# Attention on one core: key tiles turned and multiplied in pairs, reciprocal sums spread through a DRAM row

## The reference

```python
q = concat([q_nope, q_rope])          # (1, 8 heads, 2048, 128 + 64)
k = concat([k_nope, k_rope])          # (1, 8 heads, 2304, 128 + 64): latent and context keys
v                                     # (1, 8 heads, 2304, 128)
s = einsum('bhqd,bhkd->bhqk', q, k) / sqrt(192)
p = softmax(s, axis=-1)
o = einsum('bhqk,bhkd->bhqd', p, v)
y = (o * silu(gate)) @ w_o
```

## Time and profile before

| | us |
|---|---|
| median of 3 timed runs (2950.66 to 2951.75) | 2951.46 |
| the profiled execution | 2949.36 |
| its span, from first to last instruction | 2947.6 |
| attention stage in it, first scores at 572.9, last product at 1942.4 | 1369.5 |
| PE busy over the span | 2873.8 |
| DVE, ACT, POOL busy over the span | 1918.9, 1505.9, 318.3 |

### The profile page before, as it was taken

How to read it: one execution, slowest core, us unless ns; L and a number is a source line. 1 busy time by engine, 2 the same in 40 slices (tenths; PEclk the granted TensorE clock), 3 DMA queues, 4 the chain that set the end, 5 groups by cost and what they waited for, 6 DMA issues and landing times. The chain is left out here.

```text
span 2947.6 us, 42819 instructions
## 1 busy us (share of the span) xinstructions
PE 2873.8 (97%) x14429; PEld 2390.4 (81%) x14429; DVE 1918.9 (65%) x3154; ACT 1505.9 (51%) x3103; POOL 318.3 (11%) x427
## 2 busy tenths in 40 slices
PE   6999999999999999999999999999999999999998
PEld 4888888788888888888888888878878888888787
DVE  6555645476767676776767677653347586965875
ACT  5554646455656565555656555544442323334643
POOL 0000000022122212212221222110000000000000
PEclk9999999999999999999999999999989999999999
DMA  7557564611211211021111211145442333344663
GB/s 272 203 201 261 180 220 159 234 53 34 76 44 43 56 60 57 26 77 44 60 39 60 60 33 54 33 143 171 157 152 78 112 103 101 108 125 132 221 197 119
DMA packets 220342, 335.92 MB, mean 114 GB/s; under 512 B 70080, under 2 KB 131152, under 8 KB 218832
## 3 DMA queue, kind: packets, MB, share of 16 engines
q1 hardware_dynamic: 215504, 324.63, 33.9%
q10 hardware_dynamic: 4608, 8.39, 0.7%
HBM read 235.31 MB, written 97.66 MB: 113 GB/s over the span
## 5 line engine op out<-in xcount | busy, mean ns | idle before, releaser
L1324 DVE TENSOR_TENSOR at_ptlo<-at_T,at_pthi 128x512 fp32r<-128x512 f32 x576 | 396.9, 690 | 304.2 <-ACT at_pthi L1202 301.2
L1186 ACT ACTIVATE at_prob<-at_S,at_nmax 128x512 f32<-128x512 f32 x634 | 407.4, 658 | 343.8 <-DVE at_nmax L1300 322.4
L1202 ACT ACTIVATE at_pthi<-at_T 128x512 fp32r<-128x512 f32 x576 | 349.0, 608 | 208.7 <-PE at_T L1068 208.7
L1289 DVE TENSOR_REDUCE at_mx<-at_S 128x1 f32<-128x512 f32 x634 | 390.6, 631 | 73.8 <-PE at_S L1041 70.7
L1068 PE MATMUL at_T<-ident,at_prob 128*128 128x128 f32 x2304 | 346.5, 273 | 2.6 <-DVE at_ptlo L1324 2.6
L1068 PEld LDWEIGHTS at_T<-ident,at_prob 128*128 128x128 f32 x2304 | 279.9, 141 | 68.1 <-DVE at_ptlo L1324 11.5
L197 PE MATMUL ci_ps<-h1hi,ci_whi 128*128 128x512 f32 x768 | 300.7, 392 | 5.3 <-DVE h1lo L2307 5.3
L198 PE MATMUL ci_ps<-h1lo,ci_whi 128*128 128x512 f32 x768 | 300.0, 391 | 0.0
L199 PE MATMUL ci_ps<-h1hi,ci_wlo 128*128 128x512 f32 x768 | 299.8, 390 | 0.0
L197 PE MATMUL at_O<-at_pthi,at_vhi 128*128 128x512 f32 x576 | 270.1, 469 | 0.6 <-DVE at_og L1338 0.5
L1036 PE MATMUL at_S<-at_khi,at_qhi 128*128 128x512 f32 x634 | 246.1, 388 | 13.0 <-ACT at_prob L1186 10.2
(11 more groups left out here) (294 smaller groups left out, 5818.3 us busy)
## 6 DMA issues: line engine op xcount, KB each, us to landing
fr_w<-in_w_front SPq DMA_DIRECT2D x75, 512.0 KB, 4.3
at_wmod<-in_w_mod SPq DMA_DIRECT2D x32, 512.0 KB, 3.6
ci_band<-in_bands SPq DMA_DIRECT2D x40, 320.0 KB, 3.5
cv_w<-in_cv_w_in SPq DMA_DIRECT2D x24, 512.0 KB, 4.7
fr_w<-in_w_front SPq DMA_DIRECT2D x24, 384.0 KB, 4.0
values<-fr_ob SPq DMA_DIRECT2D x36, 256.0 KB, 2.9
at_vst<-values SPq DMA_DIRECT2D x8, 1152.0 KB, 8.1
fr_w_mod<-in_w_modr SPq DMA_DIRECT2D x17, 512.0 KB, 5.6
```

Source lines behind the costliest of these rows:

```text
L1186: nc.scalar.activation(prob[:, j % 2, i, k], bank(h, j, i, c)[:, 0:k.stop - k.start], ACT.Exp, scale=SCALE, bias=nmax[:, i % 2:i % 2 + 1], ...
L1202: nc.scalar.activation(dst, T[:, (n + SLOTS * j) % 2], ACT.Copy).then_inc(s_hi, 1)
L1289: nc.vector.tensor_reduce(mx[:, i % 2, c:c + 1], bank(h, j, i, c)[:, 0:k.stop - k.start], AXX, ALU.max).then_inc(s_mx, 1)
L1324: nc.vector.tensor_tensor(ptlo[:, kt % 3], T[:, (n + SLOTS * j) % 2], pthi[:, kt % 3].bitcast(F32), ALU.subtract).then_inc(s_lo, 1)
```

## The change

The `den` slot is gone, and so are the diagonals on DVE and POOL, the two matmuls and ACT's copy. `rl` now keeps the four query tiles' reciprocals of a block, and SyncE writes them to a row of 512 numbers in DRAM and, when that has landed, reads the row back to all 128 partitions of `den`. The 18 key tiles are handled as nine pairs: eight transposes in a row (two banks of `T`), then the six products of the pair before. The rings `pthi` and `ptlo` have four tiles where they had three. Pairs stand after chunks 1, 2 and 4 for i = 0 and after chunks 1 and 4 for the other tiles. `sb("apart", ...)` only keeps the addresses of what follows.

```diff
+    PAIRS_AFTER = ((1, 2, NCHUNK - 1),) + ((1, NCHUNK - 1),) * (QT - 1)
+    RING = 4
@@ SyncE
+        def spread_reciprocals(sp, h, j):
+            b = index(h, j)
+            sp.wait_ge(s_recip, b * QT + QT)
+            if not (isinstance(b, int) and b == 0):
+                sp.wait_ge(s_gden, b)
+            sp.dma_start(net.rl_row.rearrange("a (i p) -> p (a i)", p=P), rl[:, j % 2],
+                         allow_slow_non_contiguous=True).then_inc(s_rlst, 16)
+            sp.wait_ge(s_rlst, b * 16 + 16)
+            sp.dma_start(den[:], net.rl_row[0:1, :].to_broadcast([P, BLK])).then_inc(s_den, 16)
...
                     load_gate(sp, nh, nj)
+                spread_reciprocals(sp, h, j)
                 if last and j == 1:
@@ TensorE
-                        if c < len(ns) - TAIL:
-                            step(h, j, ns[c])
-                        if i == 0 and c == TAIL + 1:
-                            values(h, j, 0)
-                    for n in ns[-TAIL:]:
-                        step(h, j, n)
+                        if c in PAIRS_AFTER[i]:
+                            pair(h, j, first_pair[i] + PAIRS_AFTER[i].index(c))
+
+            def pair(h, j, p):
+                for n in (2 * p, 2 * p + 1):
+                    transposes(h, j, n)
+                if p:
+                    for n in (2 * p - 2, 2 * p - 1):
+                        values(h, j, n)
+                elif not (isinstance(h, int) and h == 0 and j == 0):
+                    for n in (NKT - 2, NKT - 1):
+                        values(*((h, j - 1) if j else (h - 1, NBH - 1)), n)
@@ ScalarE, the tail
+                    a, b = tail(i)
+                    high(h, j, a)
                     if with_scores:
                         exponential(nh, nj, i, 0)
-                    high(h, j, ns[-2])
+                        exponential(nh, nj, i, 1)
+                    high(h, j, b)
                     if with_scores:
-                        exponential(nh, nj, i, 1)
                         exponential(nh, nj, i, 2)
-                    high(h, j, ns[-1])
@@ VectorE
-                nc.vector.reciprocal(rl[:, i % 2:i % 2 + 1], lsum[:, i % 2, 7:8]).then_inc(s_recip, 1)
-                dve.wait_ge(s_recip, t + 1)
-                nc.vector.tensor_scalar(dghi[:, j % 2, i * P:(i + 1) * P], net.ident[:], rl[:, i % 2:i % 2 + 1], None,
-                                        ALU.mult).then_inc(s_dghi, 1)
+                nc.vector.reciprocal(rl[:, j % 2, i:i + 1], lsum[:, i % 2, 7:8]).then_inc(s_recip, 1)
@@ GpSimd
-                pool.wait_ge(s_hi, h * (SLOTS * NBH) + (slots.index("den") + 1 + SLOTS * j))
+                pool.wait_ge(s_den, b * 16 + 16)
-            def diagonal_low(h, j, i):
...
```

More of the change, by code:

```diff
@@ L862, in attention @@
     NBH = SEQ // BLK
[L864 to L867, removed]
+    PAIRS_AFTER = ((1, 2, NCHUNK - 1),) + ((1, NCHUNK - 1),) * (QT - 1)
+    first_pair = [sum(len(x) for x in PAIRS_AFTER[:i]) for i in range(QT)]
+    assert sum(len(x) for x in PAIRS_AFTER) == NKT // 2
+    KEARLY, KHIGH = 2, 3
+    RING = 4
     with nc.cleanup_on_exit(), ExitStack() as st:
@@ L882, in attention @@
         lsum = sb("lsum", [P, 2, 8])
[L883 to L886, removed]
+        rl = sb("rl", [P, 2, QT])
+        sb("apart", [P, 5 * 256 - 2 * (QT - 1)])
         den = sb("den", [P, BLK])
@@ L922, in index, with ring, middle, tail @@
             return h * NBH + j
+        def ring(j, n):
+            return (n + NKT * j) % RING
+        def middle(i):
+            return [range(2 * p, 2 * p + 2) for p in range(first_pair[i], first_pair[i] + len(PAIRS_AFTER[i]) - 1)]
+        def tail(i):
+            p = first_pair[i] + len(PAIRS_AFTER[i]) - 1
+            return 2 * p, 2 * p + 1
         def opening(h, j):
@@ L1107, in phase @@
                 for i in range(QT):
-                    ns = list(range(cuts[i], cuts[i + 1]))
                     for c in range(NCHUNK):
@@ L1143, in _ @@
                 phase(HEADS - 1, j, j + 1 < NBH)
-            for n in (SLOTS - 2, SLOTS - 1):
+            for n in (NKT - 2, NKT - 1):
                 values(HEADS - 1, NBH - 1, n)
@@ L1362, in phase @@
                                 denominator(h, j, QT - 1)
-                        if j == NBH - 1 and with_scores and i == 0 and c == 0:
-                            k_low(h + 1, NCHUNK - 1)
+                            if j == 0 and i == 1:
+                                v_low(h, VC - 1)
+                            if j == NBH - 2 and not last and i == QT - 1:
+                                for k in range(KEARLY):
+                                    k_low(h + 1, k)
                     if with_scores:
@@ L1370, in phase @@
                         v_low(h + 1, i - 2)
-                    low(h, j, ns[-2])
-                    if j == NBH - 1 and i >= 2 and with_scores:
-                        denominator(nh, nj, i - 1)
-                    low(h, j, ns[-1])
+                    for n in tail(i):
+                        low(h, j, n)
                     if j == NBH - 2 and not last and i == QT - 1:
```

145 lines of the change are left out of this document (44 added, 101 removed).

## The result

The changed kernel takes 2959.78 us (median of 9 runs, 2954.23 to 2964.15) against 2949.37 us of the kernel before (9 runs, 2948.82 to 2951.75): a ratio of 1.003, with a 95% interval of 1.0022 to 1.0038. It is slower, by 10.4 us, where I had forecast 13.4 us less than 2949.4; it lies above my whole range. The profiled execution took 2961.52 us, of which 2959.4 are its span. The kernel before was timed again with each group of runs; its medians lie between 2948.6 and 2950.43, so that some 1 us between groups means nothing.

What follows compares the result with a forecast made beforehand. Attention was taken as bound by TensorE's instruction stream. From the profiled 2949.4: - 14.7 - 3.5 + 3.0 = 2934.2 us, plus 2.1 for the timed median gives 2936.3, stated as 2936; range 2928 to 2942 (60%).

Steps and rivals of the forecast that it cites:

- The two `den` matmuls: On TensorE's path: removing both saves 0.46 us in each of 32 slots, 14.7 us.
- the 3.5 us of the exponentials: Scores waiting for exponentials at i = 0 of a head's last block: 0.5 us saved in 7 heads, between 0 and 5.
- Pairs in place of single steps: TensorE's fewer changes between transposes and products: taken as 0, with ends of 0 and 23 us gain.
- rival 1: Going from transposes to products really costs 0.08 us, so 23 us more go: 2913 us; chance 13%.
- The tail: Transposes and products before the next scores: a `high` ahead of the exponential on ACT costs nothing, with 0.02 us cover.
- rival 2: ACT's first copy in the tail delays exponentials and scores in 124 tails: 2948 us at 0.1 us beyond the edge; 16%.
- The pair after chunk 1: Its transposes come 4.6 us after the tail's first; the tail's last `low` is done at 3.8, so no cost.
- the DRAM row: Reciprocals written to DRAM and read back: no cost in 31 blocks, since `gden` is wanted one block later.
- The DRAM row's write: SyncE's small write of 128 x 4 pieces of 4 bytes: taken as 3 us, between 2.7 and 10.8.
- Rival 3: The small write takes 10 us or more, hidden in steady blocks but not the last: 2944 us; chance 8%.
- The last block: `og_raw` issued behind the small write makes ACT and PE wait: 3 us lost in sum, between 0 and 11.
- Rival 4: The clock falls in runs of eight transposes; one in ten falling costs 25 us: 2961 us; chance 3%.

Runs made afterwards that it cites:

- Run 7: run 3 plus, in every block, two 512-column matmuls with overwritten results ahead of the transposes of key tile 8: 2932.36 us.
- Run 6: Kernel before with the DRAM row for `den` and run 3's two edits, single steps, three buffers, POOL's gate product also behind `q_low`: 2935.23 us.
- run 5: run 3, with pairs, and POOL's gate product also made to wait until `q_low` is finished: 2921.12 us.
- run 12: Changed kernel with the reciprocals written in SBUF's order, 128 pieces of 16 bytes instead of 512 of 4 (output not the reference's): 2927.13 us.
- run 1: Changed kernel with one wait added: POOL's modulation products start only after `q_low` of the block before: 2935.11 us.
- run 9: Kernel before with POOL's modulation products formed one block early, ahead of the gate product, so they lie beside `q_low`: 2978.89 us.
- run 3: Changed kernel with POOL's modulation products behind `q_low` and, in the last block, SyncE's loads ahead of the reciprocals' row: 2921.99 us.

## Why the prediction was wrong

**The two `den` matmuls, -14.7: right.** Run 7 puts 14.0 us of the attention back, though only 10.4 of the median. Run 6, the kernel before without the slot, in single steps and with nothing of POOL beside `q_low`, has its last `at_og` 19.2 us sooner than before, where this term and the 3.5 us of the exponentials together gave 18.2; by the medians of its group it is 15.2 us faster (2935.23 against 2950.43).

**Pairs in place of single steps, 0: wrong in size, 14.1 by the medians and 11.5 in the attention's own time.** That is about midway between my 0 and the end at 23. The row I set against it still holds: eight transposes and six products take 2.26 us (1221.04 to 1223.30 in the changed kernel), as in single steps, so that the 0.08 us behind the transposes are no gain and rival 1 names the wrong place. What I did not cost is the way back to the scores. In 27 blocks of the traces of runs 5 and 6, the second matmul of a score group of 512 columns starts 0.230 us after the first with pairs and 0.242 with single steps, and the other three distances add 0.006. With 16 such groups in a block that is 16 x 0.018 = 0.29 us; transposes and products with what follows them add 0.10. Together they are the 0.38 us by which the blocks differ (41.76 against 41.38), some 12 us in 32 blocks. The first distance is longest where a group stands behind work of another kind: 0.239 behind a product (13 groups in a block of run 6) and 0.314 behind transposes (1), against 0.229 behind scores (2); with pairs 0.233 behind a product (9) and 0.227 behind scores (7). Single steps come back to scores 14 times in a block and pairs 9, so rival 1 was right that a change of kind costs something. Why it does, no run shows.

**The tail, 0: right.** Of rival 2's many waits there is nothing: 4.3 us in 4. The waits at i = 0 are gone as said.

**The pair after chunk 1, "covered by 0.8 us or more": the step that failed.** It is covered as long as the tail's last `low` comes by 3.8 us. In VectorE's order `q_low` stands ahead of that `low`, and the term does not name it. At its old two times 0.69 us it would have been harmless: in run 12 it ends 2.4 us after the tail's first transpose (1199.45 to 1201.85). In the changed kernel it ended 5.0 us after it (1209.91 to 1214.91), and the transposes of the next pair, due at 4.6, started at 5.8. And under **the DRAM row** I wrote that in 31 blocks it does not matter, because `gden` is wanted only a block later. I asked who waits for `gden` and not what is queued behind POOL's wait for it, nor beside what it would then run. There stand some 5 us of products, which in the kernel before ran from 1199.94 us on, and were done before `q_low`. That neglected queue, and with it the length of `q_low`, is what failed. Shown by run 1 (24.7 us back by moving them alone), run 9 (29.6 us lost by moving them onto `q_low` in the kernel before) and run 12 (gone when `den` comes sooner). Every step of the move is in the first trace: the order of POOL's program, and when the reciprocals come.

That the two engines block each other was to be read ahead of time as well. By the trace, the second instruction of `q_low` ends 0.55 us behind the POOL product it met, and that product took 2.37 us in place of the 1.91 in run 12. The Trainium skill says so in "SBUF — State Buffer", Who interferes with whom: a VectorE instruction with two inputs in SBUF contends with a GpSimd instruction that reads SBUF, and the contention is an exclusive lock. The traces agree, also in whom it spares: `low`, with one input in PSUM, keeps its 687 to 690 ns in all these kernels, and the 34 that lay wholly beside a POOL instruction in the changed kernel took 0.69 us as well.

**The DRAM row's write, 3 us: wrong in size, 8.4.** It was within its bounds (2.7 to 10.8), nearer to the end that I had not taken: four times the nearest row goes by the number of pieces, and run 12 shows that the cutting into pieces is what counts, since the same 2 KB in a quarter of them take 1.4 us. Rival 3 spoke of the last block alone.

**The last block, +3: wrong in size, 11.9** (36.60 us against 24.66). The mechanism was right: ScalarE waits for `og_raw`. The read of the row was issued 9.5 us behind the write (1914.29 to 1923.80), where I had counted 3.4, and `og_raw` behind it took 7.0 us to land in place of 5.5; PE stood for 11 us, and came back at half clock (0.53), which I did not cost at all. With the loads first the block takes 25.74 us, 1.1 more than before. PE's wait for the modulation column is gone, as said. Rival 4 (the clock in runs of eight transposes) did not occur: 1.00 between 640 and 1900 us in every trace.

**The sum again, by the last `at_og`.** For it the forecast was 1942.84 - 14.7 - 3.5 + 3.0 = 1927.6. Measured, step by step between traces: 1942.84, less 19.2 (run 6), less 11.5 for the pairs (run 5), plus 0.9 for the gate product back beside `q_low` (run 3), plus 11.1 for the last block (run 1), plus 25.8 for the meeting, is 1949.9, the changed kernel. Behind the attention another 4.8 us are lost: 6.1 in the convolutions, less the 1.3 gained ahead of them. Two of the 2936 us were noise from the start: I added 2.1 for medians above the profiled execution, and over nine runs of before there is no such difference (2949.37 and 2949.36). Whether the 4 to 6 us that the convolutions took more in both traces of the changed kernel are chance is not settled: the ranges with and without the row point to the row, run 12's 791.9 us against it.

## What to carry to other kernels

When an engine gets a new wait, write down what stands behind it in its queue and find the moment at which that will now run: here an engine busy for 8% of the time set the pace, through the one neighbour that it locks out. Place such work by a wait on what it must not meet; that was 25 us for one wait. And a small transfer that others queue behind is priced by its pieces, not its bytes (8.4 us and 1.4 us for the same 2 KB): count them, and keep urgent loads ahead of it. When two medians differ by a few us, look at the stage that the edit touches: the pairs are 14.1 us by the medians and 11.5 where they act.

## What I had not expected of the hardware

- 2 KB from SBUF to DRAM took 8.4 us in 512 pieces of 4 bytes and 1.4 us in 128 of 16.
- VectorE's subtraction of two tensors in SBUF, 0.69 us alone, took up to 2.40 us beside GpSimd's instructions, and GpSimd's product of 1.91 took 2.37.
- A load of 1 MB issued 0.4 us behind a 256 KB read of one DRAM row to all partitions landed after 6.5 to 7.7 us in four traces, and after 5.4 to 5.7 in the ten where it was not.
- A stage whose instructions do not change took 791.9 to 799.0 us in 14 traces. At one place of it TensorE pauses for 0.6 to 2.7 us for nothing that the profile shows, and in five traces the granted clock falls behind that pause, which costs another 1.6 us.
